# A decoder trunk on one core: the first chunk behind a norm split into old residual and addend

## The reference

```python
for layer in range(DEPTH):
    h = rms_norm(r, norm_mix_pre[layer])
    proj = h @ w_in[layer]                  # latents, q, k, v, gates
    ...
    mix = (sigmoid(g_a) * out_a + sigmoid(g_b) * out_b) @ w_out[layer]
    r = r + rms_norm(mix, norm_mix_post[layer])
    h = rms_norm(r, norm_ffn_pre[layer])
    gu = h @ w_gate_up[layer]
    ff = (silu(gu[..., :D_FF]) * gu[..., D_FF:]) @ w_down[layer]
    r = r + rms_norm(ff, norm_ffn_post[layer])
...
def rms_norm(x, gain):
    return x * rsqrt(mean(x * x, axis=-1) + 1e-6) * gain
```

## Time and profile before

| | us |
|---|---|
| Median of 3 runs | 800.08 (799.9 to 800.8) |
| The profiled execution | 799.78 |
| Its span, from the first to the last instruction | 798.0 |
| TensorE busy | 788.9 (99%) |
| VectorE busy | 576.1 (72%) |
| ScalarE busy | 451.9 (57%) |
| POOL busy | 134.9 (17%) |

### The profile page before, as it was taken

The page is one execution under the profiler, slowest core; times in us unless marked ns, Lnnn a source line. Parts: engine busy times, 40 slices in busy tenths (PEclk is TensorE's granted clock), DMA queues, the critical chain, the costliest instruction groups (busy, mean ns, idle before and its releaser), DMA issues.

```text
span 798.0 us, 16819 instructions
## 1 busy us (share of the span) xinstructions
PE 788.9 (99%) x6300; PEld 764.8 (96%) x6300; DVE 576.1 (72%) x964; ACT 451.9 (57%) x766; POOL 134.9 (17%) x146
## 2 busy tenths in 40 slices
PE   9999999999999999999999999999999999999997
PEld 9999899999999999999999999999999999999885
DVE  6899787587787666666668987876877977676432
ACT  7657655665565454455556567656755754545331
POOL 0212000224421111101122202001243211111000
PEclk9999999999999999999999999999999999999999
DMA  9767333256166455355644674332462665657951
GB/s 340 263 214 237 127 107 106 80 159 210 56 204 216 162 174 174 112 168 169 210 154 136 204 243 135 108 108 102 159 211 73 220 215 182 191 178 197 274 134 53
DMA packets 55531, 134.87 MB, mean 169 GB/s; under 512 B 20896, under 2 KB 21536, under 8 KB 55344
## 3 DMA queue, kind: packets, MB, share of 16 engines
q1 hardware_dynamic: 38608, 131.43, 51.1%
q10 hardware_dynamic: 16864, 2.62, 1.9%
HBM read 131.93 MB, written 2.10 MB: 168 GB/s over the span
## 4 chain that ended last, share of the span: by engine, by line
PE 96%; ACT 2%; issue 1%; DVE 1%; DVEq 0%
PE bank L1316 24%; PE bank L1318 23%; PE bank L1317 23%; PE bank L1350 4%; PE bank L1737 3%; PE bank L1738 3%; PE bank L1736 3%; PE bank L1341 2%; PE bank L1591 2%; PE bank L1560 2%; PE bank L1610 1%; PE bank L1435 1%; PE bank L1409 1%; ACT gates L659 1%; PE bank L1562 1%
## 5 line engine op out<-in xcount | busy, mean ns | idle before, releaser
L871 DVE TENSOR_TENSOR w_lo<-w_raw,w_hi 128x1024 fp32r<-128x1024 f32 x246 | 333.0, 1357 | 35.9 <-ACT w_hi L436 33.0
L1316 PE MATMUL bank<-h_hi,w_hi 128*128 128x272 f32 (+1 forms) x1200 | 346.4, 289 | 0.0
L1318 PE MATMUL bank<-h_hi,w_lo 128*128 128x272 f32 (+1 forms) x1200 | 343.3, 286 | 0.0
L1317 PE MATMUL bank<-h_lo,w_hi 128*128 128x272 f32 (+1 forms) x1200 | 342.4, 285 | 0.0
L436 ACT ACTIVATE w_hi<-w_raw 128x1024 fp32r<-128x1024 f32 x246 | 258.6, 1056 | 125.6 <-PE bank L1318 53.5
L1316 PEld LDWEIGHTS bank<-h_hi,w_hi 128*128 128x128 f32 x1200 | 226.6, 189 | 0.5
L1318 PEld LDWEIGHTS bank<-h_hi,w_lo 128*128 128x128 f32 x1200 | 226.6, 189 | 0.0
L1317 PEld LDWEIGHTS bank<-h_lo,w_hi 128*128 128x128 f32 x1200 | 226.6, 189 | 0.0
L836 POOL TENSOR_TENSOR pbuf<-sbuf,ubuf 128x272 f32<-128x272 f32 (+1 forms) x44 | 38.5, 874 | 205.6 <-DVE ubuf L1246 204.0
L769 POOL TENSOR_TENSOR acc<-acc,sq 128x272 f32<-128x272 f32 (+1 forms) x45 | 47.6, 1058 | 131.4 <-ACT sq L449 131.2
L1246 DVE TENSOR_TENSOR ubuf<-bank,rstd_h 128x272 f32<-128x272 f32 (+1 forms) x44 | 18.9, 430 | 44.8 <-PE bank L1318 44.8
(11 more groups left out here) (238 smaller groups left out, 1213.3 us busy)
## 6 DMA issues: line engine op xcount, KB each, us to landing
w_raw<-weights SPq DMA_DIRECT2D x216, 512.0 KB, 3.8
w_raw<-weights SPq DMA_DIRECT2D x16, 384.0 KB, 3.4
w_raw<-weights SPq DMA_DIRECT2D x16, 320.0 KB, 2.9
w_first<-first_weights SPq DMA_DIRECT2D x2, 512.0 KB, 7.2
x_tok<-x_rows SPq DMA_DIRECT2D x1, 1024.0 KB, 11.0
turn<-y ACTq DMA_DIRECT2D x4, 256.0 KB, 7.2
r_tok<-turn ACTq DMA_DIRECT2D x8, 128.0 KB, 5.5
out_tokens<-o_tok SPq DMA_DIRECT2D x4, 256.0 KB, 2.1
```

Of the source, the lines that this page charges most:

```text
L871: dve.tensor_tensor(w_lo[:, n % RING, :], w_raw[:, n % RAW, :], w_hi[:, n % RING, :].bitcast(f32), ALU.subtract).then_inc(lo_ready, 1)
L1316: pe.matmul(dst, wh, hi, start=first, stop=False)
L1317: pe.matmul(dst, wh, lo, start=False, stop=False)
L1318: return pe.matmul(dst, wl, hi, start=False, stop=last)
```

## The change

The change splits chunk 0's activation behind each of the three boundaries by linearity: `(r_new) * g = r_old * g + (y * 1/root * g_post) * g`. The two terms have high and low parts of their own: `old_hi`, `old_lo`, `new_hi`, `new_lo`. So TensorE multiplies chunk 0's weights twice, once with the old residual and once with the addend.

- Ahead of the boundary, behind tile 5: ScalarE makes `old_hi` and `y_first = y * g_post * g` (`old_high`), VectorE behind tile 6 `old_lo` (`old_low`).
- TensorE's filler goes. In its place: the old products of tiles 0 and 1 ahead of the spread, a second spread into bank 6 behind the first, and the old products of tile 2. Those of tile 3 come behind the new high products.
- VectorE makes `new_hi = y_first * 1/root` from bank 7 in one instruction. ScalarE copies the second spread into SBUF (`root_inv`), since POOL makes from it `new` and `new_lo`, and adds chunk 0 into `r` (`first_add`), with a `first_part` that VectorE makes.
- ScalarE makes the high parts in the order 1, 2, 3, 4, 5, 0, 6, 7 and squares chunks 0 to 3 in one go behind high part 3, once POOL has made `r` of chunk 0. VectorE starts with chunk 1 and makes chunk 0's low part behind the last add.
- At the start, three products of gains (`both_gains`, `[128, 1]` each).

```diff
--- before.py
+++ after.py
 DOWN_SPLIT = (6, 6, 5, 5)
 HALF = D_MODEL // 2
+CHUNK_ORDER = [1, 2, 3, 4, 5, 0, 6, 7]
 TAIL = 8
 SLOT = 8 * P
...
         def boundary_from(b):
             return N_META if b >= 2 * DEPTH - 1 else 0
+
+        def nxt(b):
+            return (G_FFNPRE, b // 2) if b % 2 else (G_MIXPRE, b // 2)
+
+        def first_gain(b):
+            g, l = nxt(b)
+            return gain[:, l, g:g + 1]
+
+        def made_before(b, c):
+
+            return KC * b + (CHUNK_ORDER.index(c) if b else c)
...
                 n = heads * len(token_chunks(t0))
                 act.activation(std[K % 2][:, 0:n], ps[bank][:, col:col + n], ACT.Sqrt, bias=eps, scale=1.0 / width).then_inc(norm_std, 1)
+            def old_high(b):
+
+                t0 = boundary_from(b)
+                act.activation(old_hi[:, t0:], r[:, 0, t0:], ACT.Copy, scale=first_gain(b)).then_inc(old_hi_ready, 1)
+                if b == 1:
+                    act.wait_ge(gains_ready, 1)
+                act.activation(y_first[:, t0:], y[:, 0, t0:], ACT.Copy, scale=both_gains[:, b - 1:b]).then_inc(y_first_ready, 1)
+
             def boundary(b, K, g, l):
                 t0 = boundary_from(b)
-                for c in range(KC):
-                    act.wait_ge(r_ready, KC * (b - 1) + c + 1)
+
+                def high(c):
                     act.activation(hh[:, c, t0:], r[:, c, t0:], ACT.Copy, scale=gain[:, l, g + c:g + c + 1]).then_inc(h_hi, 1)
-                    square(K, c, r[:, c, t0:], t0)
+
+                act.wait_ge(second_spread, b)
+                act.activation(root_inv[:, t0:], ps[6][:, 64 + t0:64 + TOK], ACT.Copy).then_inc(root_copied, 1)
+                for c in CHUNK_ORDER:
+                    if c == 0:
+                        high(0)
+                        continue
+                    act.wait_ge(r_ready, (KC - 1) * (b - 1) + c)
+                    high(c)
+                    if c == 3:
+                        act.wait_ge(r_first_ready, b)
+                        for d in range(4):
+                            square(K, d, r[:, d, t0:], t0)
+                    if c > 3:
+                        square(K, c, r[:, c, t0:], t0)
             for i, (a, b) in enumerate(PIECES[0:2]):
...
                     square_tile(K0 + POST_MIX, TL("out") + m, m)
+                    if m == 5:
+                        old_high(2 * l + 1)
                 root(K0 + POST_MIX, 7, D_MODEL, t0)
                 boundary(2 * l + 1, K0 + PRE_FFN, G_FFNPRE, l)
...
                     pool.tensor_tensor(acc[:, K % 2, t0:], acc[:, K % 2, t0:], sq[:, plan.sq_place[K, c], t0:], ALU.add).then_inc(sq_added, 1)
+
+            def first_add(b):
+
+                t0 = boundary_from(b)
+                pool.wait_ge(root_copied, b)
+                pool.tensor_tensor(new[:, t0:], y_first[:, t0:], root_inv[:, t0:], ALU.mult).then_inc(new_ready, 1)
+                pool.wait_ge(new_ready, b)
+                pool.wait_ge(new_hi_ready, b)
+                pool.tensor_tensor(new_lo[:, t0:], new[:, t0:], new_hi[:, t0:].bitcast(f32), ALU.subtract).then_inc(new_lo_ready, 1)
+                pool.wait_ge(first_part_ready, b)
+                pool.tensor_tensor(r[:, 0, t0:], r[:, 0, t0:], first_part[:, t0:], ALU.add).then_inc(r_first_ready, 1)
             def rope_add(l, i, dst, src):
...
             def lo_part(b, c, g, l, t0):
-                dve.wait_ge(h_hi, KC * b + c + 1)
+                dve.wait_ge(h_hi, made_before(b, c) + 1)
                 dve.scalar_tensor_tensor(out=hl[:, c, t0:], in0=r[:, c, t0:], scalar=gain[:, l, g + c:g + c + 1],
                                          in1=hh[:, c, t0:].bitcast(f32), op0=ALU.mult, op1=ALU.subtract).then_inc(h_lo, 1)
...
                 parts, made = (tres, rstd_q), {}
+                dve.wait_ge(y_first_ready, b)
+                dve.tensor_tensor(new_hi[:, t0:], y_first[:, t0:], ps[7][:, 64 + t0:64 + TOK], ALU.mult).then_inc(new_hi_ready, 1)
+
+                def first_product():
+                    dve.scalar_tensor_tensor(out=first_part[:, t0:], in0=y[:, 0, t0:], scalar=gain[:, lp, gp:gp + 1],
+                                             in1=ps[7][:, 64 + t0:64 + TOK], op0=ALU.mult, op1=ALU.mult).then_inc(first_part_ready, 1)
+
                 def product(c):
-                    if c >= 2:
-                        dve.wait_ge(r_ready, KC * (b - 1) + c - 1)
+                    if c >= 3:
+                        dve.wait_ge(r_ready, (KC - 1) * (b - 1) + c - 2)
                     ins = dve.scalar_tensor_tensor(out=parts[c % 2][:, t0:], in0=y[:, c, t0:], scalar=gain[:, lp, gp + c:gp + c + 1],
                                                    in1=ps[7][:, 64 + t0:64 + TOK], op0=ALU.mult, op1=ALU.mult)
                     if c < KC - 1:
@@ -914,19 +981,25 @@
...
                     dve.tensor_tensor(r[:, c, t0:], r[:, c, t0:], parts[c % 2][:, t0:], ALU.add).then_inc(r_ready, 1)
-                product(0)
-                add(0)
                 product(1)
                 add(1)
-                for c in range(2, KC):
+                product(2)
+                add(2)
+                first_product()
+                for c in range(3, KC):
                     product(c)
                     lo_part(b, c - 2, *nxt(b), t0)
                     add(c)
+                lo_part(b, 0, *nxt(b), t0)
                 lo_part(b, KC - 2, *nxt(b), t0)
                 lo_part(b, KC - 1, *nxt(b), t0)
-            def nxt(b):
-                return (G_FFNPRE, b // 2) if b % 2 else (G_MIXPRE, b // 2)
+            def old_low(b):
+
+                t0 = boundary_from(b)
+                dve.wait_ge(old_hi_ready, b)
+                dve.scalar_tensor_tensor(out=old_lo[:, t0:], in0=r[:, 0, t0:], scalar=first_gain(b),
+                                         in1=old_hi[:, t0:].bitcast(f32), op0=ALU.mult, op1=ALU.subtract).then_inc(old_lo_ready, 1)
             dve.memset(x_sum, 0.0)
             dve.memset(eps, EPS).then_inc(const_ready, 1)
...
+                for b in range(1, 2 * DEPTH):
+                    l, g = (b - 1) // 2, G_MIXPOST if b % 2 else G_FFNPOST
+                    step(dve.tensor_tensor(both_gains[:, b - 1:b], gain[:, l, g:g + 1], first_gain(b), ALU.mult))
                 after(steps[0])
-                dve.memset(idle, 0.0).then_inc(const_ready, 1)
+                dve.memset(idle, 0.0).then_inc(gains_ready, 1)
             for l in range(DEPTH):
                 t0, K0 = T0(l), NORMS * l
...
                     to_y(K0 + POST_MIX, TL("out") + m, m)
+                    if m == 6:
+                        old_low(2 * l + 1)
                 recip(K0 + POST_MIX, t0)
                 dve.wait_ge(norm_bc, K0 + POST_MIX + 1)
                 residual(2 * l + 1, K0 + POST_MIX, G_MIXPOST, l, t0)
@@ -1273,6 +1351,8 @@
...
-            def first_tiles(tiles, ready):
-
-
-                if tiles[0][1]:
-
+            def old_part(b, tiles, start=True):
+
+                pe.wait_ge(old_lo_ready, b)
+                slot_ready(tiles[-1][1])
+                for t, n, _, t0 in tiles:
+                    if start:
+                        bank_free(t)
+                    dst = ps[bank_of(t)][:, t0:TOK]
+                    pe.matmul(dst, w_hi[:, n % RING, 0:P], old_hi[:, t0:], start=start, stop=False)
+                    pe.matmul(dst, w_lo[:, n % RING, 0:P], old_hi[:, t0:], start=False, stop=False)
+                    pe.matmul(dst, w_hi[:, n % RING, 0:P], old_lo[:, t0:], start=False, stop=False)
+
+            def first_tiles(tiles, ready, b=0):
+
+
+                if b:
+                    bank_free(tiles[3][0])
+                else:
                     slot_ready(tiles[-1][1])
-                bank_free(max((t for t, *_ in tiles), key=lambda t: -1 if plan.before[t] is None else plan.before[t]))
+                    bank_free(max((t for t, *_ in tiles), key=lambda t: -1 if plan.before[t] is None else plan.before[t]))
                 hi_sem, lo_sem, base = ready
+                def part(q, k, src, t0):
+
+                    if b and k == 0:
+                        return (new_hi, new_lo)[q][:, t0:]
+                    return src[k][q]
+
+                def part_ready(q, k):
+                    if b and k == 0:
+                        pe.wait_ge((new_hi_ready, new_lo_ready)[q], b)
+                    else:
+                        pe.wait_ge((hi_sem, lo_sem)[q], (made_before(b, k) if b else base + k) + 1)
+
                 def low(k):
-                    pe.wait_ge(lo_sem, base + k + 1)
+                    part_ready(1, k)
                     for t, n, src, t0 in tiles:
-                        mm = pe.matmul(ps[bank_of(t)][:, t0:TOK], w_hi[:, n % RING, k * P:(k + 1) * P], src[k][1],
+                        mm = pe.matmul(ps[bank_of(t)][:, t0:TOK], w_hi[:, n % RING, k * P:(k + 1) * P], part(1, k, src, t0),
                                        start=False, stop=k == KC - 1)
                         if k == KC - 1:
```

(30 more changed lines are left out.)

29 lines of the change are left out of this document (21 added, 8 removed).

## The result

The changed kernel takes 802.99 us in the median (six executions of seven 802.67 to 803.43), the kernel before 800.2 beside it: a ratio of 1.0032, with a 95% interval of 1.0021 to 1.0042. It is slower by 2.8 us, where 800.4 was forecast within 798.8 to 802.0. The profiled execution took 802.67 with a span of 800.9, 2.9 more than the 798.0 before.

The account below looks back on a forecast made before the run. TensorE, busy 99%, bounds the kernel. Boundary 1: -1.02 + 0.38 + 0.10 + 0.56 = +0.02; three boundaries +0.2, ahead of them +0.15, total +0.35 us: 800.4 us from the median 800.08, range 798.8 to 802.0.

Parts of the forecast that it names:

- The hand-off: At boundary 1, VectorE writes chunk 0's high part itself, so TensorE starts at 207.15 instead of 208.17: -1.02 us.
- The three old products: Chunk 0's old products for the fourth tile, standing behind the new high ones on TensorE: +0.38 us.
- Chunk 1: At boundary 1, chunk 1 has no margin and POOL's first new product runs beside VectorE's add: +0.10 us charged.
- rival (c): Each of POOL's three new instructions blocks a VectorE add or h_lo until it ends: +0.8 per boundary, 802.8 us; chance 0.05.
- The squares in one go: ScalarE's squares 0 to 3 in a row wait for POOL and delay high part 4: +0.56 us at boundary 1.
- Ahead of the boundary: ScalarE's two extra instructions between the squares of tiles 5 and 6 delay POOL's addition: +0.15 us, between 0 and 0.5.
- at nothing: VectorE's extra old_lo (0.50) and layer 0's three tiny products of gains, charged nothing as VectorE is busy 72%.
- (a): ScalarE isn't held, so each boundary keeps -0.64, in all -1.9: 798.2 us; chance 0.12.
- (d): The change doesn't bring TensorE forward; only the +0.38 remain, three times: 801.2 us; chance 0.05.
- (b): POOL's instructions behind the boundary take 1.22 us instead of 0.97 and decide: +2.1, 802.2 us; chance 0.10.

Follow-up runs that it names:

- last attempt: Changed kernel with squares one by one, no shift, chunk 0 last, VectorE making `new` and `new_lo` behind chunk 3's add: 800.15 us, ratio 0.9999.

## Why the prediction was wrong

**The hand-off** was right: -1.02 forecast, -0.99 measured (3.30 against 4.29). **The three old products** came as +0.38.

**"Chunk 1" is the step that failed.** It charged +0.10 between bounds of 0 and 0.12, where chunk 1 cost 0.55 at boundary 1, by the duration of one `h_lo` beside POOL, and gave the full lock (rival (c)) a chance of 0.05, because "the 0.62 of the earlier trace rows speaks against it". A duration was the wrong thing to read: it depends on how late the second instruction started. Read by ends, the same row is a case of full blocking like the others:

| held instruction | starts | POOL's instruction ends | held one ends | behind it |
|---|---|---|---|---|
| before, `h_lo` | 212.44 | 212.75 | 213.06 | 0.31 |
| after, add 1 | 207.72 | 208.42 | 208.72 | 0.30 |
| before with POOL's product, add 0 | 207.51 | 208.04 | 208.35 | 0.31 |
| `new` behind add 1: add 2 | 209.29 | 209.77 | 210.07 | 0.30 |
| last attempt, add 7 | 216.14 | 216.84 | 217.14 | 0.30 |

The 0.30 is the time that the held instruction takes once POOL is done, and it goes with its size. In the kernel before, the 28 low parts that start beside a reading POOL instruction end 0.28 to 0.30 us behind it, and the splits of 1024 columns, 1.22 us otherwise, end 1.08 behind it, as here (217.96 to 219.04):

```profile
216.94 1.02 POOL L769 TENSOR_TENSOR acc<-acc,sq 128x272 f32<-128x272 f32 x1 [0.33 <-ACT sq L449]
217.26 1.78 DVE L871 TENSOR_TENSOR w_lo<-w_raw,w_hi 128x1024 fp32r<-128x1024 f32 x1
```

Started early in POOL's instruction, the same lock costs 0.56 instead of 0.12. I had the 0.31 in hand and took it for a partial overlap. The Trainium skill's rule ("SBUF — State Buffer", section "Who interferes with whom") is borne out here in each part: the later of the two waits in full, a POOL instruction that only writes holds nobody (0.44 beside a memset), and VectorE's product with one input from SBUF isn't held (208.64, 0.48 us, beside `new_lo`). At boundary 1 chunk 1 starts 5.20 us behind the sums where 4.83 was forecast with the charge. The experiment without `new` prices POOL's two instructions at 0.56 a boundary, which is what chunk 1 cost.

**The squares in one go** were right in mechanism: waits of 0.43, 0.61 and 0.51 us at chunk 4 where 0.56 and 0.2 more at boundary 2 were forecast. By starts the one of boundary 1 cost 0.70, since the sum had no term for the slower matmuls behind a wait. Taking the squares apart gave back 0.29 a boundary, not 0.56. Chunk 1's wait doesn't hide the rest: without POOL's two instructions, where that wait is absent, the same edit gave 0.29 too (47.97 to 47.09). The rest goes into the new wait ahead of chunk 3. I forecast +0.2 for the three boundaries together and got +2.0, of which 1.68 went with POOL's two instructions.

**Ahead of the boundary** +0.15 was forecast, and nothing came at boundary 1 or 3: at boundary 1 POOL's last addition ended at 203.93, TensorE came at 204.13. The extra 0.9 us outside was a term that the sum didn't have (0.7 for the shift), and one taken "at nothing" (0.2 for the products of gains): the cover that I named, VectorE being busy 72%, is a mean over the span, and at 88 us VectorE is the chain.

**Of the rivals** (c) came true, with its mechanism, its sign written down ahead (an add of over 0.6 us) and nearly its time, 802.8 for 802.99; its 0.8 a boundary was 0.6, and the rest was made up by what lay outside, which it didn't name: that the time fits so closely is luck. (a) and (d) fell: ScalarE is held, and TensorE does start earlier. (b) fell: POOL's additions here take 0.88 us each (three in 2.63).

## What to carry to other kernels

Before giving POOL an instruction, list VectorE's instructions with two SBUF inputs that will lie beside it, and let each do its work only behind POOL's end (0.3 us of it for 272 columns, 1.1 for 1024); judge overlap by ends, not by durations. A hand-off made shorter is worth only as much as the next engine in the relay has room for: here 1 us came free, and one lock, or two VectorE instructions more, used most of it up. Work called small is free only if the queue it joins isn't the chain at that very place, and an edit that changes an allocation should be timed with the allocation alone.

## What the runs showed of the hardware

- A VectorE instruction with two SBUF inputs that starts behind a reading POOL instruction ends behind it by a time that goes with its own size: 0.30 to 0.31 us in the five places of the table (272 columns), 1.08 for a split of 1024 columns at 217.26 before. Beside POOL's memsets an add takes its usual 0.44, and a product with one of its inputs in PSUM its usual 0.48 beside a reading POOL instruction.
- Moving the tensors behind `small` by 32 bytes made a stretch of matmuls with no waits 0.4% slower (124.85 to 125.4 ns from start to start; 231.7 to 233.0 in the last down projection), and the whole kernel by a ratio of 1.0012 (1.0003 to 1.0021), at a granted clock of 1.00. It shows where TensorE reads `ff_hi` and `ff_lo`, which moved, in all six kernels with the move and in none of the eight without. Why their place matters wasn't tried and stays open.
- Behind a wait TensorE's next eight matmuls of 272 columns took 1.08 to 1.12 us from first start to the start behind the eighth, without one 0.99 to 1.02, at the same granted clock (boundary 1 before and after).
